# Gates applied to expert results before they are stored, and gathers that add onto the residual rows: one core, a two-layer diffusion step

## The chip, the cores and the metric

The kernel runs on one core of one Trainium2 chip. The metric is the device time of one execution in microseconds (us). All data are 32-bit floats.

## The reference, cut to what matters

A step of a hybrid backbone over 640 tokens of width 1024: 128 context tokens and 512 latent tokens. Layer 0 mixes tokens by attention, layer 1 by a state-space scan, and after each mixer stands a mixture of experts (MoE). Each sub-layer has shift, scale and gate rows of its own, one set for context tokens and one for latent tokens.

```python
def moe(h, router_w, router_b, w_gate, w_up, w_down):
    scores = jax.nn.sigmoid((t @ router_w).astype(F32))
    ...                       # top-1 group of four, then the top-2 experts inside it
    w = w / jnp.sum(w, axis=-1, keepdims=True)
    gates = jnp.sum(jax.nn.one_hot(idx, N_EXPERTS, dtype=F32) * w[..., None], axis=1)
    hg = jnp.einsum('td,edf->tef', t, w_gate)
    hu = jnp.einsum('td,edf->tef', t, w_up)
    act = jax.nn.silu(hg) * hu * gates[..., None].astype(t.dtype)
    out = jnp.einsum('tef,efd->td', act, w_down)
```

The layer then computes x = x + gate_row * out, where gate_row (1024 values) belongs to the layer and to the kind of token. So each token takes results of two of 16 experts, each times a weight of its own, their sum times the gate row, added onto the residual.

## The kernel before, in words

The five blocks of 128 tokens lie in SBUF: X holds the residual rows, H the normed rows. The layers run one after the other, and in each the MoE goes in four stages.

**Routing.** PE computes the logits of a block as soon as it is normed (`logit_columns`, L640). The first of these waits for `s_x >= 48`, that is for the latent rows, the router's matrix RW and the router's bias RB, which SP loads (L440, L441) behind a store that sets the whole table `slot_rows` to zero (L438). In the first layer these logits stand between the products of the attention's output projection (L897), in PE's order of instructions. VectorE (DVE) then works out the top experts, the weights, and for each token the two slots in the table (L1810 to L1890): expert e owns 96 slots, what goes beyond them goes to surplus slots of 64. Then DVE makes a selection matrix (PICK, L1874 and L1878) from which PE forms the first pack's rows without the table (`first_rows`, L921), and last of all the weights of the two choices, `gate2` (L1893 to L1895).

**Scatter.** GpSimd (POOL) writes each token's row of H to its two slots, 10 indirect DMAs (L2177).

**Packs.** A pack is 128 slots; there are 12 (PACKS), and after them a loop of `trips` rounds of two surplus packs. For each pack PE turns the rows (`rows_turned`, L931), multiplies them by the experts' gate and up matrices (`gate_up`, L947), turns the activations (`act_turned`, L956) and multiplies by the down matrix (`down`, L968). ScalarE (ACT) copies the turned rows out of PSUM (`rows_out`, L1383), applies SiLU (L1392), copies the turned activations (L1396), copies the pack's result out of PSUM (`result_out`, L1402) and stores it over the pack's slots in `slot_rows` (L1404); it also loads the rows of later packs (L1388, L1438). DVE only multiplies gate by up (`activations`, L1901). PE's order within a pack is: turn the rows of the pack after next, turn the activations, gate_up of the next pack, down of this one. `down` of a pack waits until the result of the pack before has left PSUM (`ycopy`). SP streams the experts' weights in a ring of five.

**Return.** When both buffers' stores have landed (`yst`), POOL gathers each token's two results from `slot_rows` into ten buffers GY (L2191), both choices of a block one after the other. ACT multiplies the first by its weight (L1465); DVE's `combine` adds the second times its weight (L1913), multiplies by the gate row MB[1][:, 2] (L1914) and adds onto X (L1915). In layer 0, ACT then squares the block and takes the root (L1448, L1449), DVE scales it into H (L1920), PE turns it (L614), ACT and DVE apply scale and shift to four column groups each (L1456, L1927), and PE makes the step products (L1020) and then the scan layer's first products (L1044). SP starts the weights for those when the first block's gathers have landed (`gat[0]`, L553 and L558). In layer 1 SP stores each block of X as output (L598), and the program ends.

```python
def trips_of(eng, l):
    return eng.value_load(npi[0:1, l:l + 1], min_val=1, max_val=MAXTRIPS)
...
if t == 0:
    pe.wait_ge(s_x, 48)
```

## Time and profile before

| | us |
|---|---|
| median of 3 runs | 1627.12 |
| lowest and highest run | 1623.88, 1633.46 |
| the profiled execution's own time | 1622.67 |
| its span, first to last instruction | 1620.9 |
| mean granted TensorE clock, share of full speed | 0.951 |

The rows below are of the profiled execution. Times in them count from its first instruction. PE is TensorE, PEld its weight loads, SPq and ACTq are queues that issue DMAs, L numbers are lines of the kernel before. "x" is a count of instructions.

### The profile page before, as it was taken

To read this page: it belongs to the slowest core of one execution; us is meant where nothing else is said; L and a number is where in the kernel's file an instruction comes from. 1 tells how busy PE (TensorE), PEld (TensorE's weight loads), DVE (VectorE), ACT (ScalarE), POOL (GpSimd) and SP (SyncE) were. 2 spreads that over 40 slices of the span, in tenths; PEclk is the share of its full clock that TensorE was granted. 3 is DMA by queue.
4 is the path that set the end of the run, shared out by engine and by line. 5 is a ranking of instruction groups with operands and counts; after the bars stand their busy time and mean duration, and the time that the engine had idled before them with its cause. 6 is when DMAs were issued, how large, how long until landed. Compare 5 with 4: busy or idle time off the path is not lost.

```text
span 1620.9 us, 18712 instructions
## 1 busy us (share of the span) xinstructions
PE 1449.0 (89%) x7371; PEld 730.3 (45%) x7371; DVE 588.7 (36%) x926; ACT 561.5 (35%) x1233; POOL 180.4 (11%) x179
## 2 busy tenths in 40 slices
PE   6998799999969999498899899899889999799980
PEld 3444354444444333274455455455455444433330
DVE  1234556652550000363445445445452133400004
ACT  4112444441112222344573573573570001122212
POOL 0112000000011000300410410410410100200002
PEclk9998999999979999779999999999998999799995
DMA  9503666469179999713233233233045020899985
GB/s 347 215 1 110 225 197 229 157 201 383 81 281 363 412 418 406 257 39 121 76 106 104 80 103 104 79 104 105 26 170 207 14 104 36 350 393 419 407 343 207
DMA packets 121330, 323.27 MB, mean 199 GB/s; under 512 B 7814, under 2 KB 37206, under 8 KB 110998
## 3 DMA queue, kind: packets, MB, share of 16 engines
q1 hardware_dynamic: 100396, 260.33, 43.8%
q0 software_dynamic: 8496, 31.17, 5.1%
q10 hardware_dynamic: 12352, 30.58, 4.8%
q8 instruction: 60, 0.98, 0.2%
q14 instruction: 26, 0.21, 0.0%
HBM read 279.05 MB, written 42.99 MB: 199 GB/s over the span
## 4 chain that ended last, share of the span: by engine, by line
PE 79%; DVE 10%; ACT 4%; DMA 4%; issue 3%; SPq 0%; POOL 0%; ACTq 0%; DVEq 0%; POOLq 0%
PE ps L947 12%; PE ps L1044 10%; PE ps L1204 9%; PE ps L1099 8%; PE ps L734 6%; PE ps L968 6%; PE ps L1046 3%; PE ps L897 3%; PE ps L681 3%; PE ps L808 2%; PE ps L824 2%; PE ps L1183 2%; PE ps L1175 2%; PE ps L931 2%; DVE mem L2009 1%
## 5 line engine op out<-in xcount | busy, mean ns | idle before, releaser
L947 PE MATMUL ps<-mem 128*32 128x512 f32 (+1 forms) x1408 | 198.2, 594 | 2.0 <-ACT mem L1383 1.6
L1044 PE MATMUL ps<-mem 128*128 128x512 f32 x384 | 171.1, 599 | 0.0
L1204 PE MATMUL ps<-mem 128*128 128x512 f32 x320 | 141.6, 602 | 2.3 <-issue 1.9
L1099 PE MATMUL ps<-mem 128*128 128x512 f32 x320 | 140.7, 593 | 0.3 <-ACT mem L1573 0.3
L1901 DVE TENSOR_TENSOR mem<-ps,mem 128x256 f32<-128x256 f32 x28 | 11.9, 425 | 335.1 <-ACT mem L1392 335.1
L1971 DVE SCALAR_TENSOR_TENSOR mem<-mem 128x642 f32<-128x642 f32 x96 | 92.6, 965 | 87.6 <-ACT mem L1497 85.0
L947 PEld LDWEIGHTS ps<-mem 128*32 128x32 f32 (+1 forms) x1408 | 59.6, 117 | 123.0 <-issue 122.9
L1044 PEld LDWEIGHTS ps<-mem 128*128 128x128 f32 x384 | 72.0, 192 | 82.0 <-issue 81.5
L734 PE MATMUL ps<-mem 128*128 128x512 f32 x240 | 106.4, 600 | 1.9 <-DVE mem L1675 1.9
L968 PE MATMUL ps<-mem 128*32 128x512 f32 (+1 forms) x704 | 102.0, 595 | 4.3 <-ACT mem L1396 4.3
L1533 ACT ACTIVATE mem<-mem,small 128x128 f32<-128x128 f32 x320 | 95.1, 391 | 24.5 <-DMA mem<-cum_rows 24.5
L1204 PEld LDWEIGHTS ps<-mem 128*128 128x128 f32 x320 | 61.1, 193 | 77.6 <-issue 77.0
L1099 PEld LDWEIGHTS ps<-mem 128*128 128x128 f32 x320 | 59.3, 190 | 67.4 <-issue 67.0
L1319 ACT ACTIVATE mem<-ps,small 128x512 f32<-128x512 f32 x64 | 43.6, 681 | 95.0 <-DVE small L1701 95.0
L808 PE MATMUL ps<-tab,mem 128*128 128x128 f32 x336 | 54.7, 286 | 19.6 <-ACT mem L1331 9.5
L734 PEld LDWEIGHTS ps<-mem 128*128 128x128 f32 x240 | 45.5, 193 | 55.8 <-issue 55.8
L897 PE MATMUL ps<-mem 128*128 128x512 f32 x160 | 69.7, 593 | 0.0
L1392 ACT ACTIVATE mem<-ps 128x256 f32<-128x256 f32 x28 | 10.7, 383 | 155.9 <-PE ps L947 155.9
L808 PEld LDWEIGHTS ps<-tab,mem 128*128 128x128 f32 x336 | 38.1, 144 | 55.9 <-issue 32.7
L968 PEld LDWEIGHTS ps<-mem 128*32 128x32 f32 (+1 forms) x704 | 28.6, 117 | 70.2 <-issue 67.5
L1402 ACT ACTIVATE mem<-ps 128x1024 f32<-128x1024 f32 x28 | 28.7, 1024 | 90.5 <-PE ps L968 90.5
L1490 ACT ACTIVATE mem<-ps 128x512 f32<-128x512 f32 x24 | 14.3, 596 | 109.2 <-PE ps L1046 109.2
(316 smaller groups left out, 2000.7 us busy)
## 6 DMA issues: line engine op xcount, KB each, us to landing
mem<-in_mod_w SPq DMA_DIRECT2D x24, 2048.0 KB, 8.3
mem<-in_expert_w_gate SPq DMA_DIRECT2D x40, 1024.0 KB, 11.2
mem<-in_expert_w_up SPq DMA_DIRECT2D x40, 1024.0 KB, 14.1
mem<-in_expert_w_down SPq DMA_DIRECT2D x40, 1024.0 KB, 16.3
mem<-cum_rows SPq DMA_DIRECT2D x40, 512.0 KB, 5.0
slot_rows<-mem ACTq DMA_DIRECT2D x28, 512.0 KB, 8.1
mem<-slot_rows ACTq DMA_DIRECT2D x26, 512.0 KB, 11.1
slot_rows<-mem SPq DMA_DIRECT2D x1, 12288.0 KB, 53.6
```

The source lines that it names most:

```text
L681: last = nc.tensor.matmul(ps[q:q + 32, bank, c0:c0 + 2 * P], COND[:, k, at:at + 32], w[:, k, 2 * P * half:2 * P * (half + 1)], start=(n == ...
L734: last = nc.tensor.matmul(ps[:, 3 * (t % 2) + j, :], HT[:, k, t * P:(t + 1) * P], WS[j][:, k, :], start=(k == 0), stop=(k == KD - 1))
L808: last = nc.tensor.transpose(ps[:, 5, j * P:(j + 1) * P], src, ident)
L897: last = nc.tensor.matmul(ps[:, 4 + 2 * (t % 2) + j, :], HT[:, k, t * P:(t + 1) * P], WS[j][:, k, :], start=(k == 0), stop=(k == KD - 1))
L947: last = nc.tensor.matmul(ps[c:c + w, 2 + j, :], XGT[j][:, k, c:c + w], GUW[l][m][:, :, k, :], start=(k == 0), stop=(k == KD - 1))
L968: last = nc.tensor.matmul(ps[c:c + w, 5 + n, :], AT[j][:, k * P + c:k * P + c + w], WD[m][:, k, n * 512:(n + 1) * 512], start=(k == 0), st ...
L1044: nc.tensor.matmul(ps[:, b, :], w[:, k, :], HT[:, k, SEQ:TOK], start=(k == 0), stop=(k == KD - 1))
L1046: last = nc.tensor.matmul(ps[:, b + 1, 0:SEQ], w[:, k, :], HT[:, k, 0:SEQ], start=(k == 0), stop=(k == KD - 1))
L1099: last = nc.tensor.matmul(ps[:, ZBANK[t], :], HT[:, k, t * P:(t + 1) * P], WZ[2 * k // KD][:, k % (KD // 2), :], start=(k == 0), stop=(k = ...
L1204: last = nc.tensor.matmul(ps[:, 4 + n % 4, :], YT[b][:, k, t * P:(t + 1) * P], w[:, k, :], start=(b == 0 and k == 0), stop=(b == 1 and k = ...
L1533: last = nc.scalar.activation(RR[cc % 2][:, d, h, :], RR[cc % 2][:, d, h, :], ACT.Identity, bias=CUM[:, cc, d, g * HG + h:g * HG + h + 1])
L1971: x = V_.scalar_tensor_tensor(AC2[st % 2], U[st % 2][:, j:j + AW], CW[:, ch, j:j + 1], AC2[st % 2], op0=ALU.mult, op1=ALU.add)
```

## The change

Seven edits belong together.

1. The table of rows gets a fifth column group: `slot_rows` has rows of 1028 values, four more than before. DVE writes into the extra values of each token's row the second choice's weight, the difference of the two weights, and the first choice's slot number. Slots count from 1, so that row 0 is unused and the subtraction of 1 (L1871) goes. Context tokens get their weights negative. All this stands before PICK in DVE's order, and `gate2` after it is gone.
2. Results go to a table of their own, `slot_results`. SP zeroes it too, ahead of the router's matrix and bias.
3. ACT copies each pack's three extra values to `gates` in `rows_out`, ahead of the copy of the turned rows, and issues a load into a row buffer only after that copy.
4. DVE makes from these values a factor row for each pack (`factor_row`): the first or second weight, whichever slot it is, times the context or the latent gate row.
5. DVE, instead of ACT, takes the pack's result out of PSUM and multiplies it by the factor row (`result`).
6. POOL's gathers add onto X in SBUF in the DMA itself: all first choices, then all second choices, each of which waits for its block's first. `combine` and ACT's multiplication are gone, and the squares of layer 0, the loads behind `gat[0]` and the output stores wait for both gathers.
7. In layer 0, ACT applies scale and shift to six of the eight column groups, DVE to two.

```diff
-        xs_d = nc.dram_tensor("slot_rows", (ROWS, D), F32, kind="Internal").ap()
+        xs_d = nc.dram_tensor("slot_rows", (ROWS + 1, WIDE), F32, kind="Internal").ap()
+        ys_d = nc.dram_tensor("slot_results", (ROWS + 1, D), F32, kind="Internal").ap()
...
-            sp.dma_start(xs_d.rearrange("(p a) (b n) -> p (a b) n", p=P, n=256),
-                         zeros.unsqueeze(1).to_broadcast([P, ROWS // P * 4, 256])).then_inc(s_rows, 16)
+            sp.dma_start(xs_d[1:1 + ROWS].rearrange("(p a) n -> p (a n)", p=P).rearrange("p (c m) -> p c m", m=WIDE // 4),
+                         zeros.unsqueeze(1).to_broadcast([P, ROWS // P * 4, WIDE // 4])).then_inc(s_rows, 16)
+            sp.dma_start(ys_d[1:1 + ROWS].rearrange("(p a) (b n) -> p (a b) n", p=P, n=256),
+                         zeros[:, 0:256].unsqueeze(1).to_broadcast([P, ROWS // P * 4, 256])).then_inc(s_rows, 16)
+            sp.dma_start(ys_d[0:1].rearrange("o (c m) -> (o c) m", m=256), zeros[0:4, 0:256]).then_inc(s_rows, 16)
+            sp.dma_start(xs_d[0:1].rearrange("o (c m) -> (o c) m", m=WIDE // 4), zeros[0:4, :]).then_inc(s_rows, 16)
             sp.dma_start(RW[:, 0:KD, :], router_w.rearrange("(p k) e -> p k e", p=P)).then_inc(s_x, 16)
             sp.dma_start(RB[:, :], router_b.partition_broadcast(P)).then_inc(s_x, 16)
...
                 load_rows(1, 1)
+                sp.dma_start(gates[:, 0, :], slots[0][:, D:D + 3]).then_inc(ES["g0"], 16)
...
-                def rows_out(t, j):
+                def rows_out(t, j, place):
                     act.wait_ge(pk["xt"], t + (dx + 1))
+                    nc.scalar.activation(gates[:, place, :], XG[j][:, D:D + 3], ACT.Copy)
                     nc.scalar.activation(XGT[j], psf[:, 0:1024].rearrange("p (k n) -> p k n", k=KD), ACT.Copy)\
...
-                def result_out(t, j, stores, pack):
-                    act.wait_ge(pk["dn"], t + 1)
-                    if not early(t):
-                        act.wait_ge(pk["yst"][j], stores * 16)
-                    nc.scalar.activation(YO[j], psf[:, 5 * 512:5 * 512 + D], ACT.Copy).then_inc(pk["ycopy"], 1)
+                def result_out(t, j, pack):
                     act.wait_ge(pk["ycopy"], t + 1)
-                    act.dma_start(slots[pack], YO[j]).then_inc(pk["yst"][j], 16)
+                    act.dma_start(results[pack], YO[j]).then_inc(pk["yst"][j], 16)
...
-                    if t < NT:
-                        act.wait_ge(ES["gat"][t], 32 * (l + 1))
-                        nc.scalar.activation(GY[t][0], GY[t][0], ACT.Copy, scale=gate2[:, 0, t:t + 1]).then_inc(ES["wa"], 1)
...
+                order(V_.tensor_scalar(wsum[:, 0:1], wsum[:, 0:1], -1.0, None, ALU.mult))
...
-                order(V_.tensor_scalar(slotm, slotf[:, :, :], 1.0, None, ALU.subtract))
-                V_.tensor_copy(sloti[:, :, :], slotm).then_inc(ES["slot"], 1)
+                V_.tensor_copy(sloti[:, :, :], slotf[:, :, :])
...
+                order(V_.tensor_tensor(of[0], spot.unsqueeze(1).to_broadcast([P, 2, NT, NE]),
+                                       slotf[:, :, :].unsqueeze(3).to_broadcast([P, 2, NT, NE]), ALU.is_equal))
+                order(V_.tensor_tensor(of[1], of[0], weighted.unsqueeze(1).to_broadcast([P, 2, NT, NE]), ALU.mult))
+                order(V_.tensor_reduce(pairs, of[1], AX.X, ALU.add))
+                V_.tensor_copy(HX[:, :, D], pairs[:, 1])
+                V_.tensor_copy(HX[:, :, D + 2], slotf[:, 0, :])
+                V_.tensor_tensor(HX[:, :, D + 1], pairs[:, 0], pairs[:, 1], ALU.subtract).then_inc(ES["route"], 1)
...
-                for a in range(2):
-                    order(V_.tensor_tensor(mine, spot, slotf[:, a, :].unsqueeze(2).to_broadcast([P, NT, NE]), ALU.is_equal))
-                    order(V_.tensor_tensor(mine, mine, weighted, ALU.mult))
-                    order(V_.tensor_reduce(gate2[:, a, :], mine, AX.X, ALU.add))
...
+                def factor_row(j, place, first_row):
+                    order(V_.tensor_scalar(signed[:, 0:1], gates[:, place, 2:3], first_row, rowno[:, :], ALU.subtract, ALU.is_equal))
+                    order(V_.scalar_tensor_tensor(signed[:, 0:1], gates[:, place, 1:2], signed[:, 0:1], gates[:, place, 0:1],
+                                                  op0=ALU.mult, op1=ALU.add))
+                    V_.tensor_scalar(signed[:, 1:2], signed[:, 0:1], -1.0, 0.0, ALU.mult, ALU.max)
+                    order(V_.tensor_scalar(signed[:, 0:1], signed[:, 0:1], 0.0, None, ALU.max))
+                    order(V_.tensor_scalar(GROW[j], MB[1][:, 2, 1, :], signed[:, 0:1], None, ALU.mult))
+                    order(V_.scalar_tensor_tensor(GROW[j], MB[1][:, 2, 0, :], signed[:, 1:2], GROW[j], op0=ALU.mult, op1=ALU.add))
+
+                def result(t, j, stores):
+                    if not early(t):
+                        dve.wait_ge(pk["yst"][j], stores * 16)
+                    dve.wait_ge(pk["dn"], t + 1)
+                    V_.tensor_tensor(YO[j], psf[:, 5 * 512:5 * 512 + D], GROW[j], ALU.mult).then_inc(pk["ycopy"], 1)
...
                 for t in range(PACKS):
-                    activations(d0 + t, t % 2)
+                    if t + 1 < PACKS:
+                        activations(d0 + (t + 1), (t + 1) % 2)
+                    result(d0 + t, t % 2, s0 + t // 2)
+                    if t + 2 < PACKS:
+                        dve.wait_ge(pk["ycopy"], d0 + (t + 1))
+                        dve.wait_ge(pk["xtc"], d0 + (t + 2 + dx + 1))
+                        factor_row(t % 2, (t + 2) % 4, (t + 2) * P + 1.0)
...
-                def combine(t):
-                    a, b = GY[t]
...
-                    V_.tensor_tensor(X[:, t, :], X[:, t, :], b, ALU.add).then_inc(ES["x2"], 1)
...
-                for t in range(NT):
-                    if t == NT - 1:
-                        pool.wait_ge(PK["xt"], trips * 2 + packs_done(pool, l) + (PACKS + 2 + 2 * l))
-                        nc.gpsimd.tensor_tensor(mark[:, 1:2], mark[:, 1:2], mark[:, 1:2], ALU.add)
-                    for a in range(2):
-                        pool.indirect_dma_start(GY[t][a], None, xs_d, bass.IndirectOffsetOnAxis(ap=sloti[:, a, t:t + 1], axis=0))\
-                            .then_inc(ES["gat"][t], 16)
+                for a in range(2):
+                    for t in range(NT):
+                        if a == 1:
+                            pool.wait_ge(ES["gat"][t], 32 * l + 16)
+                        pool.indirect_dma_start(X[:, t, :], None, ys_d, bass.IndirectOffsetOnAxis(ap=sloti[:, a, t:t + 1], axis=0),
+                                                oob_is_err=True, compute_op=ALU.add).then_inc(ES["gat"][t], 16)
```

In the loop of surplus packs DVE makes the two factor rows at the start of each round, before its first `activations`, by the same six kinds of instruction with the two packs interleaved and a wait on a counter (`fac`) after each kind, and calls `activations` and `result` for each of the two packs. Ahead of the loop it loads `trips` as before, and in layer 1 also layer 0's `trips`, from which the counter's offset comes.

## Rows read from the trace of the kernel before

**Rows 1.** The page's busy time by engine: share of the span, instructions.
```profile
PE 1449.0 (89%) x7371; PEld 730.3 (45%) x7371; DVE 588.7 (36%) x926; ACT 561.5 (35%) x1233; POOL 180.4 (11%) x179
```

**Rows 2.** Stretch of packs, layer 0: us, PE PEld DVE ACT POOL, clock, DMA share, GB/s.
```profile
512.00:628.00 116.00, 116.00 (x904) 40.84 (x900) 3.82 (x9) 26.70 (x40) 0.00 (x0) 1.00 1.01 407
```

**Rows 3.** Issues of SP's queue in order of time: start, us, what.
```profile
351.24 0.62 SPq L438 DMA_DIRECT2D slot_rows<-mem  x1
...
397.99 0.74 SPq L441 DMA_DIRECT2D RB<-in_router_b  x1
```

**Rows 4.** DMA issues: KB, us from issue to landing.
```profile
slot_rows<-mem SPq DMA_DIRECT2D x1, 12288.0 KB, 53.6
...
RB<-in_router_b SPq DMA_DIRECT2D x1, 8.0 KB, 7.2
```

**Rows 5.** Stretches of the zero store and of routing, columns as in rows 2.
```profile
365.00:380.00 15.00, 12.68 (x71) 8.28 (x71) 4.37 (x13) 3.79 (x11) 0.00 (x0) 0.89 1.09 386
...
475.00:480.00 5.00, 5.00 (x8) 1.88 (x7) 4.56 (x24) 0.00 (x0) 0.66 (x1) 0.60 0.79 320
```

**Rows 6.** PE in order of time: the first router product.
```profile
423.67 0.64 PE L640 MATMUL ps<-mem,RW 128*32 128x128 f32 x16
```

**Rows 7.** DVE and PE in order of time, routing of layer 0.
```profile
467.98 0.49 DVE L1818 TENSOR_TENSOR mem<-mem,tab 128x320 f32<-128x320 f32 x1
...
474.68 5.82 PE L913 MATMUL ps<-mem,tab 128*128 128x512 f32 x8
...
483.70 0.22 DVE L1893 TENSOR_TENSOR mem<-mem,slotf 128x80 f32<-128x80 f32 x1
```

**Rows 8.** ACT in order of time, end of the packs of layer 0.
```profile
638.01 1.02 ACT L1402 ACTIVATE mem<-ps 128x1024 f32<-128x1024 f32 x1 [2.85 <-PE ps L968]
...
640.46 0.90 ACTq L1438 DMA_DIRECT2D mem<-slot_rows  x2
```

**Rows 9.** DVE in order of time: three kinds of 128x1024 operation, and `activations`.
```profile
394.13 1.23 DVE L1799 TENSOR_TENSOR mem<-ps,mem 128x1024 f32<-128x1024 f32 x1 [12.18 <-PE ps L897]
...
645.42 0.42 DVE L1901 TENSOR_TENSOR mem<-ps,mem 128x256 f32<-128x256 f32 x1 [15.73 <-ACT mem L1392]
...
679.54 1.28 DVE L1913 SCALAR_TENSOR_TENSOR mem<-mem,gate 128x1024 f32<-128x1024 f32 x1
...
683.44 0.75 DVE L1920 TENSOR_SCALAR mem<-mem,ssq 128x1024 f32<-128x1024 f32 x1
```

**Rows 10.** The chain that ended last, return of layer 0: start us, us, what.
```profile
667.89 0.98 POOL mem L2191
668.87 0.30 issue
669.17 5.38 DMA mem<-slot_rows,sloti
...
711.17 6.92 PE ps L1044 x16
```

**Rows 11.** ACT and PE in order of time, return of layer 0.
```profile
679.65 1.06 ACT L1448 ACTIVATE mem<-mem 128x1024 f32<-128x1024 f32 x1 [0.55 <-DVE mem L1915]
...
682.11 0.29 ACT L1449 ACTIVATE ssq<-ssq,eps 128x1 f32<-128x1 f32 x1
...
686.26 1.50 ACT L1456 ACTIVATE mem<-ps,small 128x128 f32<-128x128 f32 x4 [0.88 <-PE ps L614]
...
694.68 1.97 PE L614 MATMUL ps<-tab,mem 128*128 128x128 f32 x8 [0.58 <-DVE mem L1920]
696.44 3.51 PE L1020 MATMUL ps<-mem 128*128 128x64 f32 x16
```

**Rows 12.** The chain that ended last, return of layer 1.
```profile
1586.84 1.00 POOL mem L2191
...
1611.91 1.23 DVE mem L1915
```

**Rows 13.** DMA issues: the output stores of layer 1.
```profile
out<-mem SPq DMA_DIRECT2D x5, 512.0 KB, 3.0
```

More of the change, by code:

```diff
@@ L198, in backbone @@
         RB = sb("RB", [P, NE])
-        mark, eps = sb("mark", [P, 2]), sb("eps", [P, 1])
-        zeros = page(49.75, 256)
+        mark, eps = sb("mark", [P, 1]), sb("eps", [P, 1])
+        zeros = page(49.75, WIDE // 4)
         route = page(41, 2048)
@@ L359, in backbone, with turned_at @@
         PK = pack_sems()
+        def turned_at(t, k):
+            return (4 + t % 2) * 512 + k * P if k < 2 else (t % 2) * 1024 + (k - 2) * P
         def trips_of(eng, l):
@@ L1453, in columns @@
                     cc = min(t, 1)
-                    for k in range(KD // 2, KD):
-                        at = (t % 2) * 1024 + k * P
+                    for k in range(2, KD):
+                        at = turned_at(t, k)
                         last = nc.scalar.activation(HT[:, k, t * P:(t + 1) * P], psf[:, at:at + P], ACT.Identity,
@@ L1906, in moe, with factors_done @@
                 trips = trips_of(dve, l)
+                f0 = 0 if l == 0 else dve.snap(trips_of(dve, 0) * 6)
                 with dve.Fori(0, trips) as i:
+                    t = [dve.snap(i * 2 + d0 + (PACKS + j)) for j in range(2)]
+                    def factors_done(k):
+                        dve.wait_ge(ES["fac"], dve.snap(i * 6 + f0 + k))
                     for j in range(2):
-                        activations(dve.snap(i * 2 + d0 + (PACKS + j)), j)
-                def combine(t):
-                    a, b = GY[t]
-                    dve.wait_ge(ES["wa"], l * NT + t + 1)
-                    order(V_.scalar_tensor_tensor(b, b, gate2[:, 1, t:t + 1], a, op0=ALU.mult, op1=ALU.add))
-                    order(V_.tensor_tensor(b, b, MB[1][:, 2, min(t, 1), :], ALU.mult))
-                    V_.tensor_tensor(X[:, t, :], X[:, t, :], b, ALU.add).then_inc(ES["x2"], 1)
+                        dve.wait_ge(pk["xtc"], dve.snap(i * 2 + d0 + (PACKS + j + dx + 1)))
+                        last = V_.tensor_scalar(signed[:, 4 * j:4 * j + 1], gates[:, j, 2:3], (PACKS + j) * P + 1.0, rowno[:, :],
+                                                ALU.subtract, ALU.is_equal)
+                    last.then_inc(ES["fac"], 1)
+                    factors_done(1)
+                    for j in range(2):
+                        last = V_.scalar_tensor_tensor(signed[:, 4 * j + 1:4 * j + 2], gates[:, j, 1:2], signed[:, 4 * j:4 * j + 1],
+                                                       gates[:, j, 0:1], op0=ALU.mult, op1=ALU.add)
+                    last.then_inc(ES["fac"], 1)
+                    factors_done(2)
+                    for j in range(2):
+                        V_.tensor_scalar(signed[:, 4 * j + 2:4 * j + 3], signed[:, 4 * j + 1:4 * j + 2], 0.0, None, ALU.max)
+                        last = V_.tensor_scalar(signed[:, 4 * j + 3:4 * j + 4], signed[:, 4 * j + 1:4 * j + 2], -1.0, 0.0, ALU.mult, ALU.max)
+                    last.then_inc(ES["fac"], 1)
+                    factors_done(3)
+                    dve.wait_ge(pk["ycopy"], dve.snap(i * 2 + d0 + PACKS))
+                    for j in range(2):
+                        last = V_.tensor_scalar(GROW[j], MB[1][:, 2, 1, :], signed[:, 4 * j + 2:4 * j + 3], None, ALU.mult)
+                    last.then_inc(ES["fac"], 1)
+                    factors_done(4)
+                    for j in range(2):
+                        last = V_.scalar_tensor_tensor(GROW[j], MB[1][:, 2, 0, :], signed[:, 4 * j + 3:4 * j + 4], GROW[j],
+                                                       op0=ALU.mult, op1=ALU.add)
+                    last.then_inc(ES["fac"], 1)
+                    factors_done(5)
+                    for j in range(2):
+                        activations(t[j], j)
+                        result(t[j], j, dve.snap(i + s0 + PACKS // 2))
+                    V_.tensor_scalar(rowno[:, :], rowno[:, :], 2.0 * P, None, ALU.add).then_inc(ES["fac"], 1)
+                    factors_done(6)
@@ L1924, in columns @@
                     cc = min(t, 1)
-                    for k in range(KD // 2):
-                        at = (t % 2) * 1024 + k * P
+                    for k in range(2):
+                        at = turned_at(t, k)
                         last = V_.tensor_scalar(HT[:, k, t * P:(t + 1) * P], psf[:, at:at + P], AB[:, 1, 0, cc, k:k + 1],
```

117 lines of the change are left out of this document (65 added, 52 removed).

## The prediction

> **What bounds the kernel now.** I read the page's busy times first: PE is busy for 89% of the span, every other engine for 36% or less [rows 1]. Then the stages by stretch. Within the packs PE is busy for all of 116 us, ACT for 26.7, DVE for 3.8 (nine `activations`, 0.42 each), and the DMA engines are full at 407 GB/s [rows 2]. So work taken from ACT in the packs gives nothing, and DVE has room. PE idles at the return: 43.3 us lie between POOL's first gather and the scan layer's dense products (667.9 to 711.2) [rows 10], and 26.3 between it and the last addition in layer 1 (1586.8 to 1613.1) [rows 12]. In the chain of waits DVE's `combine` fills most of both: three passes of 1.23 to 1.28 us [rows 9, 12] for each of five blocks. The change takes these out. Last I read what SP's queue does before the first MoE. The zero store is issued at 351.2 and takes 53.6 us; the router's bias is issued behind it at 398.0 and lands 7.2 us later, at 405.2 [rows 3, 4]. The first router product starts at 423.7 [rows 6]: 18.5 us of slack.
>
> **The second zero store.** It adds 12.58 MB to the same queue, ahead of RW and RB. At the 386 GB/s of the stretch that the first one fills [rows 5], that is 32.6 us, and two tiny stores with it some 0.7. RB lands at 405.2 + 33.3 = 438.5, and L640 can't start at 423.7: PE waits 14.8 us. Behind it in PE's order are the output projections of blocks 3 and 4, which nothing else can do, so the wait is paid in full. The gate row loads are no later: the first store still ran when they were made. The clock falls in that wait, I take it: around 475 PE begins dense work at 1.2 GHz at 474.7 [rows 7], and the stretch to 480 has a mean of 0.60 [rows 5], so the clock rose to 2.4 GHz at about 479. 4.3 us at half rate lose 2.2. Sum: +17.0. If the clock held, +14.8.
>
> The first store's pieces grow from 1024 to 1028 bytes and start at odd places. No row shows such pieces. Their cost lies between nothing and a second piece for each, which would double 32.6 us. The nearest row is the store of 1024-byte pieces; I take nothing and keep the other end. By the Trainium skill (DMA: Bandwidth & Descriptors, How a descriptor splits into AXI transactions) a piece that doesn't start on a 256-byte boundary also fetches the bytes below its start; as an estimate from that page, 13% more for these, which would put RB 4 us later. No run here shows it.
>
> **Routing.** Ahead of PICK DVE gets three operations of 128x160, between 0.22 (80 values) and 0.49 (320) [rows 7], so 0.35 each with the step between them, and three tiny ones at 0.15; 0.2 goes with L1871. +1.3 per layer, on the path to `first_rows` and to the scatter alike. The negation falls into DVE's wait for PE's counts: nothing, and 0.2 without that cover. The six gate operations behind PICK had no one waiting.
>
> **Packs.** A factor row costs DVE 4 tiny operations (0.7), 0.75 and 1.28, so 2.75 with its steps; `result` 1.23 instead of ACT's 1.02 [rows 8, 9]. With `activations` DVE has 4.4 of the 12 us or so that a pack takes PE (116 us with nine `activations`). A factor row starts behind `result`, 1.3 us after `down` ends, and is over some 4 us before the next SiLU. Without that cover, each pack would pay up to 2.75. PE waits on these only at the ends: ACT's copy of the three values stands before the first `rows_out` (+0.2, below 0.4); the last regular `act_out` and the last store stand behind `result` instead of ACT's copy (+0.2 each). In the surplus loop DVE starts 1.1 us after its last `result` (ACT needed that between 639.4, behind its store's issue, and 640.5 [rows 8]); at about 640.5 it does 8 tiny operations with waits (1.0) and four of 128x1024 (4.1), to 645.6, with a few waits to 646.1, while SiLU is ready at 645.6 (645.42 before, and the 0.2) [rows 9]: +0.5, in layer 1 +1.1 for the second register load. Sum with routing: +2.4 in layer 0, +3.0 in layer 1. Bounds: 1.5 and 5 per layer. The wider rows add 0.4% to loads and scatter in a stretch where the DMA engines are full; nothing taken, up to 2 us per layer kept, since packs wait for weights at once if that ring falls behind. ACT's order is now load after copy: 1 us later for data needed two packs on, nothing.
>
> **The gathers.** A plain gather costs POOL 0.98 + 0.30 [rows 10]. Block 0's second was issued by 670.1 and landed at 674.55, 4.4 us later, of which 1.25 is 512 KB at the packs' rate and 3.2 is fixed. No row shows a DMA that adds. Its cost lies between the plain gather's (1.28 each, held by POOL) and, since the row of X must be read as well as the table's, 1 MB at 407 GB/s, 2.6 us each. I don't exclude three times (read, read, write through one path: 3.9). I take 2.6: the engines were full at one read per byte. By the Trainium skill (Collectives: The Full Stack, The bandwidth ceiling) a DMA that reduces reads two sources through the same read ring, which halves its rate; by that rule the sum is the one below, by the plain row 25 us less. No run here shows it yet.
>
> Gathers finish in order: number n (from 0) lands at G + 1.0 + 3.2 + 2.6 (n + 1). The waits of second choices on the first hold nothing up, since a backlog stands in the rings. All first choices come first, so block 0 is complete with number 5, at G + 19.8.
>
> *Layer 0.* G = 667.9 + 2.4 = 670.3, block 0 complete at 690.1 (before: X by 679.65, where ACT squares it [rows 11]). Then a square and root take 2.8 with the table load, 1.6 later on; ACT's columns are six of 0.375, 2.25; PE needs 1.97 and 3.51 a block at 1.2 GHz [rows 11]. SP's 3 MB for the scan layer now start at 690.1 too and share with the last four gathers: 5 us apart instead of 2.6, the last at about 707. From there: 1.6 + 0.9 (scale) + 1.1 + 2.3 + the last step product and what queues before it, PE at 717.2 instead of 711.2. +6.0.
>
> *Layer 1.* G = 1586.8 + 3.0 = 1589.8; number 9 alone at 1620.0, with the output stores of blocks 0 to 2 between (1.5 MB, 3.7 us) 1623.7; its own store 3.0 [rows 13], to 1626.7 instead of 1613.1 + 3.0. +10.6.
>
> **Sum.** 17.0 + 6.0 + 10.6 = 33.6. The profiled execution took 1622.7 (span 1620.9), 4.4 below the median of the runs: 1656.3, taken as 1656. From the median it would be 1661.
>
> **Rivals.**
> *The add is free (plain rate).* POOL then sets the pace. Block 0 complete at G + 11.7 = 682.0, and ACT's 3.85 a block brings PE to L1044 at 705.7 (-5.5). In layer 1 the last four gathers and five stores, 4.7 MB, end with their landing at 1613.1 (-3.0). 17.0 - 8.5 = +8.5: 1631. For: one stream in, one out. Against: full engines at one read.
> *The add costs three times.* +9 and +13 more: 1678.
> *The pieces of 1028 bytes split in two.* 32.6 us more of wait at L640: 1689. For: they cross every boundary; against: 4 bytes more.
> *Not slower: the zero stores keep out of the way.* Place: L640's wait. If both zero stores ran at over 700 GB/s, or RB weren't held behind them, it would vanish: it decides from RB landing before 423.7. With the plain rate the sum is -8.5: 1614. Against: RB was issued 46 us after its turn, so that queue is in order, and 386 GB/s is near the 407 at which the engines are full in the packs. With the doubled rate it would be +16.6.
> *It doesn't do what it says:* DVE's factor rows could come too late for SiLU in every pack. With over 7 us of free time per pack this needs them at three times their rows; small, inside the range.
>
> **How the numbers follow.** Forecast 0.50; add free 0.20; three times 0.12; split pieces 0.07; no wait at L640 0.11, half of it with the plain rate. The range goes from just under the free add, 1629, to between three times and split pieces, 1682; outside lie the 1614 case and most of the split, about 0.15. A measurement here tells 0.5%, 8 us, from no change. Slower: the forecast, three times, split, half of the free add (its +8.5 lies on the edge) and 0.05 of no wait, 0.84. Same: 0.11. Faster: 0.05.
>
> **What would show it.** The zero stores' landing near 437 and PE idle before L640 for about 15 us at a halved clock behind it; if RB lands before 424, the largest term is wrong. Gathers landing 2.6 us apart, block 0's second 19.8 us after POOL's first, not 11.7. Packs with PE busy throughout and L1402 gone from ACT. In the surplus loop, `activations` 0.5 to 1.1 us after SiLU. PE at L1044 43.3 + 3.6 us after the first gather.

## The result and the profile after

The changed kernel takes 1676.5 us against 1627.1 us, both medians of six executions: ratio 1.0301, 95% interval 1.0271 to 1.0331, or +49 us where +34 was forecast. One of the six took 5219.8 us, in a slow state, and is left out of the ratio; the median of the other five is 1675.7. The profiled execution took 1677.3 us (span 1675.3, against 1620.9), so the two traces differ by 54.4 us of span.

PE has the same 7371 matmuls. DVE is busy for 68 us more and ACT for 31 less, answering to [rows 1]:

```profile
PE 1456.8 (87%) x7371; PEld 734.3 (44%) x7371; DVE 656.5 (39%) x1086; ACT 530.5 (32%) x1237; POOL 189.1 (11%) x177
```

Issues of SP's queue in order of time (start, us, what), answering to [rows 3]:

```profile
353.90 0.68 SPq L447 DMA_DIRECT2D slot_rows<-mem  x1
354.63 66.82 SPq L449 DMA_DIRECT2D slot_results<-mem  x1
421.48 35.05 SPq L451 DMA_DIRECT2D slot_results<-mem  x1
456.57 1.10 SPq L452 DMA_DIRECT2D slot_rows<-mem  x1
457.71 1.08 SPq L453 DMA_DIRECT2D RW<-in_router_w  x1
458.84 1.16 SPq L454 DMA_DIRECT2D RB<-in_router_b  x1
460.05 1.01 SPq L466 DMA_DIRECT2D mem<-in_expert_w_gate  x1
```

A long time in this view is that of an issue held up by the transfers queued ahead of it. RB is issued at 458.8 instead of 398.0, and the first expert's weights at 460.1. PE in order of time shows who pays (the bracket is idle time and its releaser), answering to [rows 6]:

```profile
413.58 1.09 PE L637 MATMUL ps<-tab,mem 128*128 128x128 f32 x8 [2.92 <-DVE mem L1624]
...
463.70 1.08 PE L652 MATMUL ps<-mem,RW 128*32 128x128 f32 x16 [34.41 <-DMA RB<-in_router_b]
464.71 15.12 PE L909 MATMUL ps<-mem 128*128 128x512 f32 x32
```

PE stands still for 34.4 us. Then the router product takes 1.08 us (0.64 in [rows 6]) and the output projection behind it 15.12; the same 32 matmuls took 13.90 at 414.5. Stretches of the same kernel (us, busy PE PEld DVE ACT POOL, clock, DMA share, GB/s), to set beside [rows 2, 5]:

```profile
364.00:374.00 10.00, 8.68 (x47) 4.66 (x46) 4.73 (x11) 3.63 (x12) 0.00 (x0) 0.87 1.12 219
...
430.00:440.00 10.00, 0.00 (x0) 0.00 (x0) 0.93 (x1) 1.79 (x4) 0.00 (x0) 0.64 1.09 387
440.00:450.00 10.00, 0.00 (x0) 0.00 (x0) 0.00 (x0) 0.00 (x0) 0.00 (x0) 0.50 1.09 387
...
1638.00:1643.00 5.00, 0.00 (x0) 0.00 (x0) 0.00 (x0) 0.00 (x0) 4.09 (x4) 0.50 1.03 192
1643.00:1648.00 5.00, 0.00 (x0) 0.00 (x0) 0.00 (x0) 0.00 (x0) 4.09 (x4) 0.50 1.05 205
1648.00:1653.00 5.00, 0.00 (x0) 0.00 (x0) 0.00 (x0) 0.00 (x0) 4.00 (x3) 0.50 1.06 210
```

The first zero store, of 1028-byte pieces, moves 219 GB/s, the second, of 1024-byte pieces, 387. The DMA engines are as full in one as in the other. The adding gathers of layer 1 (the last three lines) keep them full too, at 192 to 210 GB/s. The packs' stretch has not changed:

```profile
557.00:673.00 116.00, 116.00 (x902) 40.74 (x896) 42.94 (x79) 18.46 (x40) 0.00 (x0) 1.00 1.01 406
```

PE is busy for 116 of 116 us; DVE has 42.9 in the place of 3.8, ACT 18.5 in the place of 26.7. POOL in layer 1 (the chain, end of layer 1) issues a gather every 1.85 us, where [rows 10] has 0.98 and 0.30:

```profile
1643.91 1.54 POOL mem L2257
1645.45 0.30 issue
1645.76 1.54 POOL mem L2257
1647.30 0.30 issue
```

And the DMA issues of that return (KB, median us to landing), the first answering to [rows 13]:

```profile
out<-mem SPq DMA_DIRECT2D x5, 512.0 KB, 8.3
mem<-slot_results,sloti POOLq DMA_INDIRECT x10, 9.7
```

**The 54.4 us stage by stage**, each the growth of the distance between two events of the two traces: ahead of the first MoE 41.6 (2.7 before SP reaches the zero store, the same work in both kernels, at a lower clock early on, on which more at the end of experiment 7; 2.9 of idle PE at L637, where the loads behind the gate rows land 2.9 us later; 34.4 for RB; the other 1.6 the halved clock behind it), routing 1.1, packs of layer 0 up to POOL's first gather 4.2, return of layer 0 up to the scan layer's dense products 1.9 (45.2 us against 43.3), from there to the routing of layer 1, the same work in both kernels, -3.1, routing 1.1, packs of layer 1 1.0, and its return up to the end 6.6 (40.7 against 34.1). In layer 0's packs, 1.1 us is the first pack of products, with a clock of 0.67 from 536 to 540, and 1.7 one `down` product of the surplus loop, with 0.57 from 692 to 694; 1.4 stay unassigned.

### The profile page after: what moved, and what is told of

Read it like the earlier page. It is cut to its first block, busy times and chain, and to the rows that moved or that the text cites. A ratio compares the mean times of both kernels' runs of the same rounds, so it can differ in the third digit from the quotient of the medians.

```text
span 1675.3 us, 18938 instructions
## 1 busy us (share of the span) xinstructions
PE 1456.8 (87%) x7371; PEld 734.3 (44%) x7371; DVE 656.5 (39%) x1086; ACT 530.5 (32%) x1237; POOL 189.1 (11%) x177
## 4 chain that ended last, share of the span: by engine, by line
PE 76%; SPq 7%; DVE 6%; issue 3%; ACT 3%; DMA 2%; POOL 1%; ACTq 0%; DVEq 0%; POOLq 0%
PE ps L959 12%; PE ps L1056 10%; PE ps L1216 8%; PE ps L1111 8%; PE ps L746 6%; PE ps L980 6%; SPq L449 4%; PE ps L1058 3%; PE ps L693 2%; PE ps L1195 2%; SPq L451 2%; PE ps L820 2%; PE ps L909 2%; PE ps L1187 2%; PE ps L836 2%
## 5 line engine op out<-in xcount | busy, mean ns | idle before, releaser
L959 PE MATMUL ps<-mem 128*32 128x512 f32 (+1 forms) x1408 | 199.3, 597 | 1.8 <-ACT mem L1395 1.8
L1056 PE MATMUL ps<-mem 128*128 128x512 f32 x384 | 171.3, 599 | 0.0
L959 PEld LDWEIGHTS ps<-mem 128*32 128x32 f32 (+1 forms) x1408 | 59.3, 118 | 123.9 <-issue 123.8
L1056 PEld LDWEIGHTS ps<-mem 128*128 128x128 f32 x384 | 72.1, 193 | 82.1 <-issue 81.7
L1930 DVE TENSOR_TENSOR mem<-ps,mem 128x1024 f32<-128x1024 f32 x28 | 34.3, 1225 | 92.2 <-PE ps L980 92.2
L1373 ACT ACTIVATE mem<-ps 128x1024 f32<-128x1024 f32 x10 | 10.2, 1025 | 145.7 <-PE ps L637 145.7
## 6 DMA issues: line engine op xcount, KB each, us to landing
mem<-in_expert_w_gate SPq DMA_DIRECT2D x40, 1024.0 KB, 10.6
```

The lines of the kernel that those rows point to most:

```text
L959: last = nc.tensor.matmul(ps[c:c + w, 2 + j, :], XGT[j][:, k, c:c + w], GUW[l][m][:, :, k, :], start=(k == 0), stop=(k == KD - 1))
L1056: nc.tensor.matmul(ps[:, b, :], w[:, k, :], HT[:, k, SEQ:TOK], start=(k == 0), stop=(k == KD - 1))
```

## Experiments

The ratios are to the kernel before on the same chip. "Return of layer 0" is from POOL's first gather to the first dense product of the scan layer (L1044, L1056 or L1057), "return of layer 1" from its first gather to the end of the span. A version ran four times where nothing else is said, ten times (`two_adds`) and twelve (`two_adds_gap`) in experiment 7; stages are read from one trace of each.

How far can one trace be trusted? Six traces have the changed kernel's gathers in layer 0 unchanged: its own, experiment 1, the three of experiment 3, and the second of experiment 4. Their return of layer 0 takes 42.4 to 46.0 us, 44.4 in the mean; that of the kernel before, in two traces, 43.3 and 43.5. The return of layer 1 takes 40.7 to 41.6 in the five of them that keep its gathers. So a difference of up to 3 us in the return of layer 0 says nothing, the +1.9 above included; one of more than 1 us in the return of layer 1 does.

**1. RW and RB ahead of the zero stores** (changed kernel).

```diff
+            sp.dma_start(RW[:, 0:KD, :], router_w...)
+            sp.dma_start(RB[:, :], router_b.partition_broadcast(P))
             sp.dma_start(xs_d[1:1 + ROWS]...)
             sp.dma_start(ys_d[1:1 + ROWS]...)
...
-            sp.dma_start(RW[:, 0:KD, :], router_w...)
-            sp.dma_start(RB[:, :], router_b.partition_broadcast(P))
```

> The changed kernel, with the router's matrix and bias loaded ahead of all zero stores; nothing else moved. Theory: PE's wait of 34.4 us at the first router product is the bias landing at 463.6 behind 25 MB of zeros, and nothing else hangs on it. Then PE does not wait there, and the time falls by 34.4 and the 1.6 us of half clock behind it, to about 1640 (13 above the kernel before). Rival: the expert weights behind the zero stores become late instead, or the clock losses are of another source; then it falls by less than 25.

Measured: 1645.7 us, 1.0141 (1.0096 to 1.0185). L652 starts at 428.1 without a wait. So 31 of the 49 us, by the medians, were the wait for 8 KB (26 by the ratios); 36 were expected. The first zero store still runs at 220 to 240 GB/s, PE still idles 3.0 us at L637, and a new wait stands in the packs of layer 0, on the side of the rival. PE in order of time there, and the chain ahead of it:

```profile
487.00 9.20 PE L933 MATMUL ps<-mem 128*128 128x128 f32 x80 [2.61 <-DVE mem L1893]
...
511.26 1.94 PE L943 MATMUL ps<-tab,mem 128*128 128x128 f32 x8 [8.05 <-issue]
```

```profile
495.19 0.96 POOL slot_rows L2244
496.46 11.03 DMA slot_rows<-mem,sloti
```

The experts' loads start at 454.3, behind the stores, instead of 398.8; the scatter meets them in full DMA engines, its last lands 11 us after its issue, and the first packs to read rows back come 8.1 us late. The forecast counted nothing for these loads.

**2. One store more in the kernel before.** The price of the second store alone, without the odd pieces.

```diff
             sp.dma_start(xs_d.rearrange("(p a) (b n) -> p (a b) n", p=P, n=256), ...)
+            sp.dma_start(ys_d.rearrange("(p a) (b n) -> p (a b) n", p=P, n=256), ...)
```

> The kernel before, with one more zero store of 12.6 MB in 1024-byte pieces ahead of the router's matrix and bias, to a table that nothing reads. Theory (the term of the prediction): 32.6 us at 386 GB/s, of which 18.5 are slack: PE waits 14 us at the first router product and loses 2 more by its clock, +16 us, ratio 1.010. Rival: the second store shares the engines with the loads of gate rows and takes longer, or PE's clock holds; 1.006 to 1.015 tells these apart in the trace, not in the time.

Measured: 1645.5 us, 1.0129 (1.0089 to 1.0169), so +21 us by the ratio and +19 by the medians, where +16 was expected. The first store moves 385 to 387 GB/s away from the gate rows' loads, the second 387 at first and 369 and 348 later on. SP's queue, and PE in order of time:

```profile
351.76 46.00 SPq L441 DMA_DIRECT2D more_rows<-mem  x1
397.81 35.89 SPq L443 DMA_DIRECT2D RW<-in_router_w  x1
433.74 1.24 SPq L444 DMA_DIRECT2D RB<-in_router_b  x1
```

```profile
441.96 1.08 PE L643 MATMUL ps<-mem,RW 128*32 128x128 f32 x16 [18.48 <-DMA RB<-in_router_b]
```

With aligned pieces PE waits 18.5 us where the forecast's term had 14.8. The other 15.9 of the 34.4 come from what the changed kernel adds to this: the odd pieces, and the two small stores, which are 1.4 of it (from the end of the second store's issue to RB's issue SP needs 37.4 us there, 35.9 here). The odd pieces give the 2.9 us at L637 too: here PE passes that line (L628) at 407.8 without a wait.

**3. What makes the odd pieces slow.** Two versions of the changed kernel's first store. In one, four stores of 1024-byte pieces write the same rows of 4112 bytes, so that pieces start on multiples of 16 bytes (the four last values of a row are zeroed later):

```diff
-            sp.dma_start(xs_d[1:1 + ROWS]..., zeros...)
+            for b in range(4):
+                sp.dma_start(xs_d[1:1 + ROWS, b * 256:(b + 1) * 256]..., zeros[:, 0:256]...)
```

> The changed kernel, with slot_rows zeroed by four stores of 1024-byte pieces, each piece starting on a multiple of 16 bytes in rows of 4112; the last 16 bytes of each row are zeroed behind the bias. Theory A: the rate of 210 to 240 GB/s of the first zero store, where the kernel before had 385, comes from the length of 1028 bytes; then it is 385 here, the bias lands 24 us earlier, PE waits about 10. Theory B: it comes from where pieces start; then the rate stays near 220 and PE waits about 34.

In the other the rows have 1056 values and pieces of 1056 bytes start on multiples of 32:

```diff
-        WIDE = D + 4
+        WIDE = D + 32
```

> The changed kernel with rows of 1056 values instead of 1028 in slot_rows, so that the zero store's pieces are 1056 bytes long and start on a multiple of 32 bytes. If starts off a 32-byte multiple are what is slow, the rate is near 385 GB/s and PE waits about 11 us at the first router product; if any piece over 1024 bytes is slow, 220 GB/s and 36 us; if starts off a 64-byte multiple are enough to slow it, between the two.

Measured, one execution each: 1660.8 and 1652.7 us. The same stretch of the two, 1024-byte pieces first:

```profile
365.00:375.00 10.00, 7.75 (x46) 5.99 (x44) 4.13 (x12) 3.83 (x11) 0.00 (x0) 0.83 1.11 327
```

```profile
365.00:375.00 10.00, 7.73 (x40) 4.54 (x42) 3.19 (x8) 3.26 (x11) 0.00 (x0) 0.83 1.09 340
```

So 327 and 340 GB/s, where the changed kernel has 219 and the kernel before 386 [rows 5]. PE waits 21.8 and 19.7 us for RB. For 1024-byte pieces neither theory had the number (385 GB/s and 10 us, or 220 and 34); the 1056-byte ones came out between the two, as expected if a start off a 64-byte multiple slows them somewhat. A third version (experiment 1, with two stores to tables that nobody reads) parts length from start; the first table has a pitch of 1088 bytes, the second of 1028:

```diff
+            sp.dma_start(far_d...[:, :, 0:257], zeros...)
+            sp.dma_start(odd_d...[:, :, 0:256], zeros[:, 0:256]...)
```

> Base: the changed kernel with RW and RB first. Behind the second zero store stand two further stores of 3.1 MB to tables of their own: first pieces of 1028 bytes that start on multiples of 64 bytes (pitch 1088), then pieces of 1024 bytes that start on multiples of 4 bytes (pitch 1028). Theory that the start of a piece sets the rate: the first goes at 340 to 390 GB/s (8 to 9 us), the second at about 220 GB/s (14 us). Theory that the length does (1028 bytes are split in two): first about 220 GB/s, second about 386 GB/s. If both count: both well under 386. The time is some 5 us longer at most than 1645.7, since nothing waits for the stores but the first scatter.

Stretches of this kernel; the first store runs in the first two lines, the second in the last two:

```profile
455.00:460.00 5.00, 3.80 (x44) 2.60 (x46) 2.65 (x3) 1.91 (x2) 0.00 (x0) 1.00 1.04 343
460.00:465.00 5.00, 1.21 (x16) 0.94 (x9) 3.47 (x4) 0.56 (x3) 0.00 (x0) 0.62 1.07 332
...
470.00:475.00 5.00, 0.09 (x1) 0.09 (x1) 4.55 (x16) 0.00 (x0) 0.00 (x0) 0.50 1.12 212
475.00:480.00 5.00, 5.00 (x15) 3.65 (x16) 3.77 (x19) 0.00 (x0) 0.00 (x0) 0.50 1.15 188
```

Pieces of 1028 bytes that start on multiples of 64 go at 332 to 343 GB/s; pieces of 1024 bytes that start anywhere on 4 bytes go at 188 to 212. It is the start that costs, not the length; why it does, no run tells. The time expected was wrong: 1677.4 us (one execution), some 32 above experiment 1 instead of 5, because the stores stand ahead of the experts' loads and the scatter, as in experiment 1 but longer: the scatter's last lands 27.9 us after its issue, and PE idles 6.6 and 25.2 us in the first packs.

**4. The price of the adding.** In experiment 1's kernel the gathers only write, so a second choice overwrites what stood in X. In the first version both layers leave out the residual addition:

```diff
-                                                oob_is_err=True, compute_op=ALU.add).then_inc(ES["gat"][t], 16)
+                                                oob_is_err=True).then_inc(ES["gat"][t], 16)
```

> Base: the changed kernel with RW and RB loaded ahead of the zero stores (1645.7 us, 1.0141 of the kernel before). The gathers here only write: the residual addition is left out, so this run prices the adding. Theory (adding halves a gather's rate and costs POOL time): a gather goes back from 1.85 to 1.28 us on POOL and from about 205 GB/s to about 400 GB/s; block 0 is complete some 11.7 us after the first gather starts instead of 19.0, the return of layer 1 gets about 6 us shorter, of layer 0 some 7 us as far as the router's wait follows block 0; sum 10 to 13 us, so about 1634 us. Rival (rate is set by the 1028-byte rows or by the table's place, not by the adding): rate stays at 205 GB/s, block 0 stays at 19 us, time within 3 us of 1645.7.

Measured: 1663.3 us, 1.0221 (1.0188 to 1.0254), far from the 1634 expected, and not the price of the adding: the missing residual changes layer 1's routing, and the trace has 7487 matmuls instead of 7371, 64 of them more in the gate product L959. Its stages can still be read. POOL is back at 0.95 us a gather; block 0 is complete 12.7 us after the first gather (11.7 expected) instead of 20.1; the return of layer 0 takes 38.3 us instead of 42.9. So the adding was left out in layer 1 alone, which lacks its residual rows in the output and has unchanged routing:

> Base: the changed kernel with RW and RB first (1645.7 us; 1.0141 of before). The adding is left out in layer 1's gathers alone, so the output lacks layer 1's residual rows and the routing of both layers stays as it was; that makes this the clean price of the adding in the last return. Theory (adding halves the rate and takes POOL 1.85 us instead of 1.28 a gather): the last gather is issued at G+12.5 instead of G+18 and lands at about G+20 instead of G+33; the span from the first gather of layer 1 to the end falls from about 40.7 us to about 32 to 34, time 1637 to 1639 us. Rival (the rate comes from the table or the rows, not from adding): no change, 1645.7 within 2 us.

Measured: 1638.0 us, 1.0082 (1.0052 to 1.0113). The return of layer 1 takes 29.0 us instead of 41.1: 12 us, 4 more than expected. The whole time fell by only 7.7, as expected; but the work between the two returns, the same in both versions, takes 5.8 us longer in this trace, so the return prices the adding and the time doesn't. Stretches of it, to set beside the three adding ones above:

```profile
1611.00:1616.00 5.00, 0.00 (x0) 0.00 (x0) 0.00 (x0) 0.00 (x0) 3.74 (x4) 0.50 0.95 309
1616.00:1621.00 5.00, 0.00 (x0) 0.00 (x0) 0.00 (x0) 0.00 (x0) 1.87 (x2) 0.50 1.03 417
```

**5. Another order of gathers** (experiment 1's kernel).

```diff
-                for a in range(2):
-                    for t in range(NT):
+                for t, a in ((0, 0), (1, 0), (2, 0), (3, 0), (0, 1), (4, 0), (1, 1), (2, 1), (3, 1), (4, 1)):
```

> Base: the changed kernel with RW and RB first (1645.7 us). Gathers in the order block 0 first, 1 first, 2 first, 3 first, then block 0 second, block 4 first, 1 second, and so on. Theory (the queue moves gathers one after another at 2.56 us each, and block 0 ends with its second): its second gather is fifth instead of sixth, so block 0 is complete 2.6 us earlier in layer 0, the last gather no earlier; about 1643 us. Rival (the wait is for the first pass as a whole, or what ends the stage is the last gather): nothing changes, 1645.7 within 1 us.

Measured: 1648.0 us, 1.0112 (1.0077 to 1.0148), the same as experiment 1. ACT in order of time shows block 0 complete 18.1 us after the first gather (686.12) instead of 20.1, but block 1 only 5.1 us behind it, 23.3 us after the first gather instead of 22.8:

```profile
704.24 1.06 ACT L1458 ACTIVATE mem<-mem 128x1024 f32<-128x1024 f32 x1 [18.22 <-DMA mem<-slot_results,sloti]
...
709.39 1.06 ACT L1458 ACTIVATE mem<-mem 128x1024 f32<-128x1024 f32 x1 [2.40 <-DMA mem<-slot_results,sloti]
```

Block 1's second choice is the seventh gather in either order, and the dense products start no earlier (44.9 us after the first gather, 42.9 in experiment 1, which is within the spread). A first block that is complete 2 us sooner gave nothing that can be seen here.

**6. Half the adding.** Experiment 1's kernel, where first choices go to a buffer, second choices are added onto them there by the gather, and DVE makes one addition a block.

```diff
+                    V_.tensor_tensor(X[:, t, :], X[:, t, :], GY[t][0], ALU.add).then_inc(ES["x2"], 1)
...
+                for t, a in ((0, 0), (1, 0), (0, 1), (2, 0), (1, 1), (3, 0), (2, 1), (4, 0), (3, 1), (4, 1)):
+                        if a == 1:
+                            pool.wait_ge(ES["gat"][t], 32 * l + 16)
```

> RW and RB first; first choices written to five buffers, second choices accumulated onto them by the gather, and one VectorE addition a block onto the residual rows (order of gathers: each block's second two places behind its first). Dose: five accumulating gathers a layer instead of ten or none. Theory (each accumulating gather costs 1.3 us more of queue and about 0.6 us more of POOL than a plain one): from first gather to the first dense expert product of layer 0 between the 35.3 us of no accumulating gathers and the 42.9 us of ten, and from first gather of layer 1 to the end between 32 and 40.7, about 36; time half way between those of two_adds and of the base, about 1637 to 1639 us. Rival (only the last of the gathers counts, or POOL does): at either end.

Measured: 1648.1 us, 1.0155 (1.0127 to 1.0182): a miss. The returns took 46.7 and 39.6 us. POOL's gathers now idle for 22.2 us of the run on landings (0 to 9 in the other versions), since a second choice stands only one gather behind its first and nothing is queued meanwhile. As a dose it says nothing; it does show that "all first choices first" is what hides that wait in the changed kernel.

**7. The gates kept, the adding on DVE.** Ten buffers, plain gathers, two plain additions a block. The gathers go block by block again, both choices of one behind each other, as in the kernel before (not shown in the cut):

```diff
+        GY = [[page(34 + 2 * t + a, D) for a in range(2)] for t in range(NT)]
...
+                def combine(t):
+                    dve.wait_ge(ES["gat"][t], 32 * (l + 1))
+                    order(V_.tensor_tensor(X[:, t, :], X[:, t, :], GY[t][0], ALU.add))
+                    V_.tensor_tensor(X[:, t, :], X[:, t, :], GY[t][1], ALU.add).then_inc(ES["x2"], 1)
...
-                        pool.indirect_dma_start(X[:, t, :], None, ys_d, ..., compute_op=ALU.add)
+                        pool.indirect_dma_start(GY[t][a], None, ys_d, ...)
```

> As the version with two additions on VectorE, but with the changed kernel's rows of 1028 values and both zero stores where they were (RW and RB first): it tells how much of the way from 1645.7 to 1622.4 us comes from the gathers and how much from the place and rate of the zero store. Theory: the gathers give about 7 to 8 us in layer 0 and 8 in layer 1, so 1629 to 1632 us; the rest, some 8 us, is the zero stores' delay to the loads of the experts and the clock. Rival (the store's place gives it all): 1640 to 1646 us.

Measured: 1629.9 us, 1.0040 (1.0020 to 1.0061), as expected. The returns take 37.8 and 31.6 us. Then the zero store of `slot_rows` is also moved behind the first two experts' loads, with rows of 1056 values:

```diff
-            sp.dma_start(xs_d[1:1 + ROWS]..., zeros...)
...
                     load_in(1, 1)
+                    sp.dma_start(xs_d[1:1 + ROWS]..., zeros...)
                     sp.wait_ge(s_op, NT)
```

> The changed kernel's gates in the evictions are kept, and its two costs taken out: the first choices and second choices are gathered without adding into ten buffers and VectorE adds them onto the residual rows (two additions a block, about 0.3 us each); RW and RB first; slot_rows has rows of 1056 values and is zeroed behind the first two experts' loads. By the theory (the 49 us are 34 of the wait for RB, about 14 of the two returns, the rest clock) this keeps the removal of the scaled additions (1.23 us twice a block) and pays no slow store before the router: 1618 to 1628 us, 0.5 per cent faster than before at best. Rival (the gates in the evictions or the extra VectorE instructions cost what the accounting put elsewhere): 1635 us or more.

> The same kernel as two_adds_gap (1622.39 us, 0.996 of before with 0.9939 to 0.998) on this chip, beside the others: by its first measurement 0.994 to 0.998 again; if that gain was chance it covers 1.000.

Measured: 1622.4 us, 0.9960 (0.9939 to 0.9980), and on another chip 1620.4 us, 0.9967 (0.9950 to 0.9984). It is faster than the kernel before by 4.6 and 3.4 us of the medians, little, but clear of the noise both times. The whole growth of the changed kernel is gone, and the gates in the evictions are still there. DVE in order of time, return of layer 0:

```profile
684.64 1.23 DVE L1989 TENSOR_TENSOR mem<-mem 128x1024 f32<-128x1024 f32 x1 [11.15 <-DMA mem<-slot_results,sloti]
685.90 1.23 DVE L1990 TENSOR_TENSOR mem<-mem 128x1024 f32<-128x1024 f32 x1
687.46 1.23 DVE L1989 TENSOR_TENSOR mem<-mem 128x1024 f32<-128x1024 f32 x1 [0.34 <-DMA mem<-slot_results,sloti]
```

A plain addition takes 1.23 us, where 0.3 was expected, and hardly less than the scaled one of before, 1.28 [rows 9]. What the gates' move saves is one of three passes a block, and ACT's multiplication. The last version makes two edits at once (the place of the store and its pitch), so which of them gave the 7.5 us isn't told. The returns take 35.3 and 32.0 us (34.1 and 31.9 in the second trace) against 43.3 and 34.1 before: 8 to 9 us and 2 us. In layer 1 the last addition waits for the last gather, which shares the DMA engines with the output stores.

What is open is a loss ahead of all this. In all three traces of this experiment PE is later than before at 350 us (by 4.7, 5.6 and 5.6), where no changed instruction has run yet, with a lower clock early on. The stretch in the kernel before, and in the second trace of the last version:

```profile
30.00:60.00 30.00, 29.45 (x134) 13.87 (x133) 2.88 (x12) 3.44 (x7) 1.41 (x3) 0.97 0.89 325
```

```profile
30.00:60.00 30.00, 28.01 (x122) 13.25 (x123) 4.01 (x19) 3.76 (x9) 0.00 (x0) 0.84 0.78 288
```

The clock is 0.84 instead of 0.97, in all three. The ten buffers are not what decides it. The changed kernel's own trace has the same loss without them, where it is the 2.7 us ahead of the zero store:

```profile
30.00:60.00 30.00, 27.71 (x125) 13.09 (x126) 4.56 (x22) 4.04 (x10) 0.00 (x0) 0.88 0.79 286
```

Experiment 6's trace, with the same ten buffers set aside, has 0.96 there and is 1.7 us late; experiment 1's is not late at all, with the code of the changed kernel up to there. Why the clock falls in some traces stays open.

## Why the prediction was right, and where it was off

The sign held, and so did the places: the wait for RB, routing, both returns. The sum of 33.6 us was too small, mostly by one term that was put at nothing. That 1676.5 still lies in the range (1629 to 1682) is in part luck: its upper end came from rivals (three times, split pieces) that did not come true. Against the profiled difference of 54.4, point by point:

- **The second zero store** (+17.0, measured 34.4 and 1.6 of clock behind it). The place and the order of the queue were right. The step that failed is the term taken at nothing: "The nearest row is the store of 1024-byte pieces; I take nothing and keep the other end." Experiments 2 and 3 show the odd pieces at 219 against 386 GB/s, and some 14.5 us of this wait and the 2.9 at L637 as theirs. The rival of split pieces had the right place but its condition (length) was wrong and its price, 32.6 us, was nearly double what was found. By the Trainium skill (DMA: Bandwidth & Descriptors, How a descriptor splits into AXI transactions) the estimate was 13% more. The runs agree with that for starts on 32 and 64 bytes (386 / 340 = 1.14), nearly for 16 (386 / 327 = 1.18), and not for starts on 4 bytes (386 / 219 = 1.76).
- **The same term, aligned** (14.8, measured 18.5 in experiment 2). RB was issued 35.7 us later, not 33.3, and PE started 8.2 us after its issue where the row of before has a landing after 7.2.
- **The clock.** The forecast charged 2.2 us behind the wait; 1.6 were lost there (2.5 in experiment 2), and again 1.1 and 1.7 at two places in the packs, and most of 2.7 early on, before any changed instruction.
- **Not foreseen:** PE's 2.9 us at L637 behind the gate rows ("The gate row loads are no later" was wrong: the last of them lands 21.4 us after its issue instead of 18.5, behind the slower store; with two aligned stores, in experiment 2, it is not late), and the experts' loads, delayed to the time of the scatter, which experiment 1 shows at 8.1 us. In the changed kernel the whole MoE came later too, and the wait at L943 isn't there; what the delay costs in it is open.
- **Routing** (+1.3, measured 1.1): right. **Packs:** the cover held, PE was busy 116 of 116 us. The surplus loop's +0.5 and +1.1 were not there: the row factors start at 683.57, right behind the last `result`, and are done by 688.7, ahead of SiLU at 689.34. The load of `trips` that ACT's trace showed as 1.1 us didn't delay DVE.
- **The adding gather** (2.6 us each against 1.28). It moves 205 to 210 GB/s, 0.5 MB in 2.5 us; in experiment 5 two of POOL's waits for landings end 2.5 us apart (699.43 and 701.91). Block 0 was complete 19.0 us after the first gather (19.8 forecast). The rivals "free" and "three times" fall. The rule cited (the Trainium skill, Collectives: The Full Stack, The bandwidth ceiling: two reads through one ring) agrees, with 210 GB/s beside the packs' 406. Whether it is that ring, or another part of the same path, no run here tells. POOL's own time per gather, 1.54 in the place of 0.95, wasn't foreseen; with the queue slower still it should have cost nothing, but no run parts the two.
- **Returns** (+6.0 and +10.6 with the shift ahead of them, +3.6 and +7.6 without; measured +1.9 and +6.6): layer 1 was right in mechanism and 1 us too high. In layer 0 the sum is as near as one trace can tell, but two readings behind it were wrong. It had the last gathers land 5 us apart and set the pace. In the chain only block 0's landing counts; behind it PE, at a mean clock of 0.64 from 737 to 760, has hardly a gap:

```profile
724.15 9.56 DMA mem<-slot_results,sloti
...
741.89 3.68 PE ps L1032 x16
745.56 1.71 PE ps L627 x8
747.27 3.31 PE ps L1032 x16
```

  And DVE's `combine` did not fill most of both returns before: in layer 0 its fifteen passes are 18.4 of the 43.3 us (18.4 of 26.3 in layer 1), and PE's products at the halved clock come behind them either way. So less was to be gained in layer 0 than the opening says.
- **No wait at L640** (1614, chance 0.11): excluded by 34.4 us of wait. The factor rows were never late.

The expected gain did exist. Of the changed kernel's return the DVE passes were gone; the adding gathers cost more than those passes had. Leaving the additions on DVE shows it: 10 to 11 us saved in the two returns, and some 4 in the whole; the 5.6 us lost early and routing's 1 us a layer take most of the rest.

## What to carry to other kernels

Before a buffer that is cleared gets wider rows or a sister, look at what stands behind the clearing store in its queue: here a wait for 8 KB cost 34 us, and two moved lines gave 31 back. Give rows of a table a pitch that keeps every piece of its clearing store on at least 16 or 32 bytes; four extra values cost more than 32 would have. Let a gather add only where the DMA engines have room; where their queue sets the pace, an addition on an idle VectorE (1.23 us for 512 KB) is cheaper than the second read (1.3 us of full engines), and it keeps the order free.

## What the runs showed of the hardware

- A store's rate by where its 1024 to 1056-byte pieces start in DRAM, with the DMA engines equally full: multiples of 1024 bytes 385 to 387 GB/s (348 to 372 toward the end of the last store), of 64 332 to 343, of 32 340 to 341, of 16 321 to 335, of 4 188 to 240.
- An adding gather of 128 rows of 4 KB: 1.54 us on POOL and about 2.5 us of full DMA engines (205 to 210 GB/s), against 0.95 and 1.25.
- An issue on SP's queue right behind a large store is held until most of the store is done: 46.0 of the 53.6 us that 12.6 MB of aligned pieces took to land, and 66.8 us behind the odd ones.
- Leaving an addition out changed the routing, and with it the number of matmuls (7487 against 7371): an ablation upstream of data-dependent work prices the data too.
